# Taking the inverse of the next head pair's key norms in the tail of a pair, on one Trainium2 core

## What is computed

```python
kk = heads(k * k_k)
kk = kk / jnp.maximum(jnp.sqrt(jnp.sum(kk * kk, axis=-1, keepdims=True)), 1e-12)
k = k * (1 + (a - 1) * k_a)
y = wkv7_scan(rh, heads(decay), kh, vh, -kk, kk * ah)
```

## Time and profile before

| | us |
|---|---|
| median of 3 runs | 2798.76 |
| the 3 runs | 2798.76, 2799.0, 2793.1 |
| the profiled execution, its own time | 2794.85 |
| its span, first to last instruction | 2793.2 |
| busy: PE, DVE, ACT, POOL | 2693.6, 1774.3, 1220.4, 243.0 |

### The profile page before, as it was taken

The page is one execution under the profiler, slowest core; times in us unless marked ns, Lnnn a source line. Parts: engine busy times, 40 slices in busy tenths (PEclk is TensorE's granted clock), DMA queues, the critical chain, the costliest instruction groups (busy, mean ns, idle before and its releaser), DMA issues.

```text
span 2793.2 us, 50423 instructions
## 1 busy us (share of the span) xinstructions
PE 2693.6 (96%) x16787; PEld 2212.4 (79%) x16787; DVE 1774.3 (64%) x2961; ACT 1220.4 (44%) x1976; POOL 243.0 (9%) x341
## 2 busy tenths in 40 slices
PE   7999999999999999999989999999999999999998
PEld 5777777777888888888877777777778888888886
DVE  5666666656655656556577777767566566565565
ACT  5444334435444434444454444444454444344443
POOL 3111111100000000000012222221000000000000
PEclk8999999999999999999999999999999999999999
DMA  6333333345655555555633333333446555555654
GB/s 198 93 92 92 92 92 95 98 137 172 194 190 186 191 194 176 199 188 188 191 108 101 99 99 94 92 93 97 151 155 201 194 180 196 188 181 202 189 183 156
DMA packets 438043, 420.25 MB, mean 150 GB/s; under 512 B 19518, under 2 KB 351952, under 8 KB 437968
## 3 DMA queue, kind: packets, MB, share of 16 engines
q1 hardware_dynamic: 434320, 412.75, 46.8%
q0 software_dynamic: 3648, 6.52, 0.8%
HBM read 417.10 MB, written 2.10 MB: 150 GB/s over the span
## 4 chain that ended last, share of the span: by engine, by line
PE 94%; DVE 3%; ACT 1%; issue 1%; DMA 0%; SPq 0%; ACTq 0%; DVEq 0%
PE gemm_bank L516 31%; PE gemm_bank L517 16%; PE gemm_bank L541 11%; PE gemm_bank L543 10%; PE gemm_bank L542 10%; PE gemm_bank L519 2%; PE mix_bank L696 2%; DVE b_zt L1157 1%; PE mix_bank L708 1%; PE mix_bank L705 1%; PE mix_bank L660 1%; PE mix_bank L726 1%; PE mix_bank L730 1%; PE mix_bank L740 1%; PE mix_bank L736 1%
## 5 line engine op out<-in xcount | busy, mean ns | idle before, releaser
L516 PE MATMUL gemm_bank<-b_hT,b_whi 128*128 128x512 f32 x3420 | 1300.8, 418 | 60.8 <-DVE b_zt L1157 51.3
L1148 DVE TENSOR_TENSOR b_wlo<-b_raw,b_whi 128x1024 fp32r<-128x1024 f32 x745 | 906.0, 1228 | 549.5 <-ACT b_whi L890 547.9
L890 ACT ACTIVATE b_whi<-b_raw 128x1024 fp32r<-128x1024 f32 x777 | 810.5, 1057 | 610.2 <-PE gemm_bank L543 424.0
L517 PE MATMUL gemm_bank<-b_hT,b_wlo 128*128 128x256 f32 x3648 | 1030.2, 286 | 0.0
L516 PEld LDWEIGHTS gemm_bank<-b_hT,b_whi 128*128 128x128 f32 x3420 | 661.6, 193 | 233.1 <-issue 70.0
L517 PEld LDWEIGHTS gemm_bank<-b_hT,b_wlo 128*128 128x128 f32 x3648 | 708.9, 194 | 14.7 <-issue 5.3
L541 PE MATMUL gemm_bank<-b_whi,b_mT 128*128 128x512 f32 x1280 | 503.2, 393 | 0.0
L543 PE MATMUL gemm_bank<-b_whi,b_mT 128*128 128x512 f32 x1280 | 498.8, 390 | 0.0
L542 PE MATMUL gemm_bank<-b_wlo,b_mT 128*128 128x512 f32 x1280 | 498.6, 390 | 0.0
L541 PEld LDWEIGHTS gemm_bank<-b_whi,b_mT 128*128 128x128 f32 x1280 | 240.4, 188 | 51.3 <-issue 1.8
L543 PEld LDWEIGHTS gemm_bank<-b_whi,b_mT 128*128 128x128 f32 x1280 | 240.4, 188 | 50.0
(11 more groups left out here) (239 smaller groups left out, 2291.3 us busy)
## 6 DMA issues: line engine op xcount, KB each, us to landing
b_raw<-in_w_up SPq DMA_DIRECT2D x256, 512.0 KB
b_raw<-in_w_down SPq DMA_DIRECT2D x256, 512.0 KB
b_raw<-in_w_in SPq DMA_DIRECT2D x384, 256.0 KB
b_raw<-in_w_out SPq DMA_DIRECT2D x60, 512.0 KB
b_raw<-in_w_in SPq DMA_DIRECT2D x8, 512.0 KB
b_xt<-in_x SPq DMA_DIRECT2D x4, 512.0 KB, 6.5
b_raw<-in_w_out SPq DMA_DIRECT2D x8, 256.0 KB
out<-b_xt SPq DMA_DIRECT2D x8, 256.0 KB, 2.3
```

Source lines behind the costliest of these rows:

```text
L516: mm(bank[b0 + b][:, :], whi[r][:, cols], pair, start=first, stop=False)
L517: m = mm(bank[b0 + b][:, 0:SEQ], wlo[r][:, cols], act[:, kt, 0, :], start=False, stop=False)
L890: f(whi[r][:, :], raw[r][:, :, :].rearrange("p a b -> p (a b)"), ACT.Copy).then_inc(hi_done, 1)
L1148: tt(wlo[r][:, :], flat(raw[r][:, :, :]), whi[r][:, :].bitcast(F32), ALU.subtract).then_inc(lo_done, 1)
```

## The change

The clamp and the reciprocal leave the head of a turn and become a function, which is called with the next pair's number at the end of the normalised y in the tail, in front of `step(8)`. For pair 0 of each layer it is called behind `key_norms`, ahead of the loop. Pair 7 of a layer calls nothing in its tail. Shapes, values and counts at run time stay as they are: 16 clamps and 16 reciprocals.

```diff
+            def inverse_norms(n):
+
+                dve.wait_ge(e["n2_root"], n + 1)
+                ts(rn[:, :], rn[:, :], 1e-12, None, ALU.max).then_inc(e["n2_max"], 1)
+                dve.wait_ge(e["n2_max"], n + 1)
+                nc.vector.reciprocal(rn[:, :], rn[:, :]).then_inc(e["n2_inv"], 1)
+
             def mixer(l, i, n, tiles, step, finish, more=True):
...
                 finish(-1)
-
-                dve.wait_ge(e["n2_root"], V)
-                ts(rn[:, :], rn[:, :], 1e-12, None, ALU.max).then_inc(e["n2_max"], 1)
-                dve.wait_ge(e["n2_max"], V)
-                nc.vector.reciprocal(rn[:, :], rn[:, :]).then_inc(e["n2_inv"], 1)
 
                 dve.wait_ge(e["w_tanh"], V)
...
-                if not more:
+                if more:
+                    inverse_norms(n + 1)
+                else:
                     attention_lo()
                 step(8)
...
                 key_norms(l, 0, PAIRS * l)
+                inverse_norms(PAIRS * l)
                 loop(dve, PAIRS - 1, turn)
```

## The result

| | before | after |
|---|---|---|
| median, us | 2794.53 | 2811.16 |
| lowest to highest, 5 runs each | 2793.1 to 2799.0 | 2810.21 to 2814.12 |
| span of the profiled execution | 2793.2 | 2812.4 |

The ratio is 1.0058, 95% interval 1.0043 to 1.0073: the change costs 16.6 us by the medians. The forecast was 2818 us, slower, 2804 to 2832.

What follows compares the result with a forecast made beforehand. PE, busy 96%, was held at pair boundaries by scaling L1157, behind POOL's splits. Profiled 2794.85 + 18.5 (tail delay) + 3.1 (clock) = 2816.4 us, with the median placed at 2818; range 2804 to 2832.

Steps and rivals of the forecast that it cites:

- PE's restart hangs on POOL's splits: At pair boundaries, PE waits for scaling L1157, held by POOL's second split, behind its first, behind DVE's slot 0 `lo`.
- 1.98 us added, 0.66 us covered, 1.32 us paid: In the tail, DVE's wait before slot 11's split covers 0.66 us; 1.32 us reaches PE at fourteen boundaries: 18.5 us.
- PE waits 0.6 us for slot 11, inside the sum: Before its last four ticks, PE waits about 0.6 us for the late split, inside the 1.32 us, not on top.
- The head's relief is worth nothing: Removing 1.98 us of DVE behind L1157 gains nothing, as `t1` has 2.88 us slack; bounds 0 and -0.66 us a turn.
- First heads: nothing: At the two first heads, POOL's split hides the later scaling: nothing, at most 0.80 us each without that cover.
- Clock, 3.1 us: Behind boundary restarts, more PE idle brings more low clock: 0.22 us each, 3.1 us in all; bounds -5 and +24.
- The base: Sum set on the profiled execution, 2794.85 us; the runs' median lay 3.9 us above it, so the forecast was 2818.
- the one in which the port changes hands: Rival at the boundary: DVE's first scaling precedes POOL's first split, PE restarts 2.1 us earlier: 2765 us; chance 3%.

Runs made afterwards that it cites:

- behind slot 11: Clamp and reciprocal in the tail between slot 11's split and y times the gate, against the changed kernel's place ahead of that split: 2825.72 us, ratio 1.0111.
- the scratch inverse: Kernel before, inverse kept in the head, plus an unused clamp and reciprocal on a free tile in the tail ahead of slot 11's split: 2813.29 us, ratio 1.0072.

## Why the prediction was right

By its own steps:

- *PE's restart hangs on POOL's splits.* Shown. Slot 0's split later moved POOL's wait and the restart with it (changed kernel, 1.26 and 1.23 us; behind slot 11, 1.94 us); 28 us of DVE work behind that split did nothing; without POOL's splits both scalings took 0.75 us and PE's idle time fell from 3.59 to 0.96 us.
- *1.98 us added, 0.66 us covered, 1.32 us paid.* Measured 1.33 us up to the start of slot 11's split. That split then took 1.16 us in place of 1.23, so 1.26 us reached POOL. 14 x 1.32 = 18.5 us was forecast; POOL's waits grew by 17.6 us. That the cover covers is shown by the clamp alone, its size by the two places in the tail, 0.68 us apart.
- *PE waits 0.6 us for slot 11, inside the sum.* There are 14 new waits. The trace counts 0.42 us of idle time, from the modelled end of the matmul before. From start to start (267.56 and 268.26 above) it is 0.70 us, where before it was 0.12 (the row below and 264.69 in the earlier trace rows): 0.58 us later. Inside the sum it was: behind slot 11 that wait was gone and the kernel slower.

```profile
264.57 0.28 PE L517 MATMUL gemm_bank<-b_hT,b_wlo 128*128 128x256 f32 x1
```

- *The head's relief is worth nothing.* Shown by the scratch inverse, within its error, and by PE's lack of waits for `t1`. It holds for this kernel alone; where DVE makes the splits the relief is worth a good part of 22 us.
- *First heads: nothing.* PE's wait there is 2.45 us in both traces at the first head of layer 0, and 1.8 us in both at that of layer 1.
- *Clock, 3.1 us.* This was the most mis-sized term. Over the fourteen stretches of 6 us behind a restart the granted clock averaged 0.657 before and 0.648 after. That is 0.009 x 6 / 0.5 = 0.11 us more of the low level, worth 0.05 us a boundary or 0.8 us in all. Over the whole span the clock was 0.979 in both. Idle grew by 0.55 us a boundary, near the 0.7 that was forecast; what failed is the slope, the low clock that more idle brings. It was read off seven places in each layer, where four and two were of the long kind, and such counts change without any change of the idle time. In the kernel with the clamp alone in the tail, PE's idle time in layer 0 was 3.45 to 3.60 us, before 3.44 to 3.60, and two of the seven stretches were of the long kind, where before four were.

```profile
339.18:345.18 6.00, 6.00 (x25) 5.18 (x26) 5.78 (x12) 3.17 (x6) 5.40 (x13) 0.72 0.45 127
407.10:413.10 6.00, 6.00 (x21) 5.18 (x22) 5.78 (x12) 2.89 (x6) 5.40 (x13) 0.59 0.42 121
```

- *The base.* The sum was set on the profiled execution, 2794.85 us, and 1.6 us were added because the median of three runs lay at 2798.76. With two more runs the kernel before stands at 2794.53. So 2818 holds 21.6 us of change on a base of 2796.4. Of the 6.8 us between it and 2811.16, 1.9 lie in the base and 5.0 in the change: 0.9 in POOL's waits, 2.3 in the clock, and 1.8 in what the terms below exceed the medians by.

The measured terms add to 17.6 + 0.8 = 18.4 us. The medians differ by 16.6 us, with 12 to 20 by the interval, and the spans of the two profiled executions by 19.2. Of these 19.2, 1.5 lie ahead of the first place that the change touches: ACT's root for pair 0 of layer 0 ended at 62.22 us before and at 63.78 after, and PE's restart in the first head moved with it, from 66.47 to 68.02.

Of the rivals, the one in which the port changes hands was worth more thought than its 3%: not as an outcome of this change, but since it named the way to the faster kernel. Its price of 2.1 us a boundary assumed that DVE in front of POOL meets no other delay. The run with POOL's splits behind the scalings, which puts DVE in front, took that delay out of PE's restart, met another one at `t1` and was 6.9 us slower than before; so the price of 2.1 us is not borne out.

## What to carry to other kernels

A busy share of 9% says nothing of what an engine costs others: here POOL's two slow splits held DVE's multiplies, and these held PE. Before work is moved into the slack of one engine, follow who waits for what stands behind it; 0.66 us of idle time in front of one wait cover 0.66 us, and what lies beyond is paid to the full if the next link has no slack. A change that loses may be half of one that wins: the inverse in the tail was worth 22 us once the tail no longer fed the lock.

## What was not expected of the hardware

A DVE instruction with one operand in SBUF was held up by POOL as well: in the run with POOL's splits behind the scalings the decay's tensor_scalar (L1254, 128x256) took 1.29 us, beginning 1.15 us ahead of the end of a split and ending 0.14 us behind it, against 0.30 us in the earlier trace rows. A reciprocal of the same shape was not: with the inverse behind slot 0's split it took 1.75 us, as always, with POOL's split all along beside it (2.36 us, as always).

```profile
265.44 2.36 POOL L448 TENSOR_TENSOR b_wlo<-b_raw,b_whi 128x1024 fp32r<-128x1024 f32 x1 [11.71 <-DVE b_wlo L1148]
265.59 1.75 DVE L1245 RECIPROCAL b_rn<-b_rn 128x256 f32<-128x256 f32 x1
```

The Trainium skill (SBUF — State Buffer, section "Who interferes with whom") names tensor_scalar among the operations that can take the shared ports; by that the trace agrees, with 1.29 us.

The clock did not follow the idle time from one kernel to the next. Behind slot 0's split PE's idle at a boundary was longer than before (3.71 to 3.79 us in place of 3.58 to 3.60 at the first six of layer 0), and yet all seven stretches of 6 us there were of the short kind, 0.72 or 0.73, where before four of seven were of the long one; over all fourteen the clock averaged 0.692 in place of 0.657, which is 0.035 x 6 / 0.5 = 0.42 us less of the low level at each, worth 0.42 x 0.5 x 14 = 2.9 us. With the inverse behind slot 11, with 4.9 us of idle, it averaged 0.614. So at idle times this close together the sign of the clock's share could not be foretold from their length. Nor does the idle time right ahead of a restart settle it alone. Where DVE makes the splits it was 0.96 us, and the low clock was gone behind the six restarts of layer 0 that were read; in the changed kernel with slot 0's split moved up it was 0.91 us at the restart whose 6 us are shown here, and the low level was there. PE had waited 2.29 us for `pair_done` just ahead of its small matmuls, 3.3 us before this restart.

```profile
206.37:212.37 6.00, 6.00 (x25) 5.21 (x26) 5.78 (x15) 3.44 (x7) 5.48 (x13) 0.72 0.44 109
```
